# Adaptive modulation chunks summed on VectorE by 32x32 transposes, and a rotary turn by lane shuffle

## The chip, the cores and the metric

The kernel runs on one core of a Trainium2 chip. The metric is device time in microseconds of that core, as the median of several executions of the whole program. The engines are called PE (TensorE), DVE (VectorE), ACT (ScalarE), POOL (GpSimd) and SP (SyncE, which issues most DMAs). SBUF is the on-chip memory, PSUM (`bank`, 8 banks of 512 fp32 columns) is where TensorE writes. All data is fp32.

## The reference, cut to what matters

Two blocks of two layers each, over a sequence of 256 tokens and a width of 1024. In block one every layer is modulated by a vector that comes from a condition `c`:

```python
cond = jax.nn.silu(c)
for l in range(DEPTH):
    mod = cond @ ada_w[l] + ada_b[l]            # (1, 1024) @ (1024, 9216)
    sh1, sc1, g1, sh2, sc2, g2, sh3, sc3, g3 = jnp.split(mod, N_MOD, axis=-1)
    hn = _modulate(_rms_norm(h, norm_g[l, 0]), sh1, sc1)
    h = h + 0.5 * g1[:, None, :] * _swiglu(hn, ffn1_w_in[l], ffn1_w_out[l])
    hn = _modulate(_rms_norm(h, norm_g[l, 1]), sh2, sc2)
    z = hn @ w_in[l]
    ...                                         # attention, convolution, gating, projection with g2
    hn = _modulate(_rms_norm(h, norm_g[l, 2]), sh3, sc3)
    h = h + 0.5 * g3[:, None, :] * _swiglu(hn, ffn2_w_in[l], ffn2_w_out[l])
```

In block two the first 16 of the 64 columns of a head are rotated by position, for queries and keys of 18 of 24 heads:

```python
x1, x2, rest = t[..., :8], t[..., 8:16], t[..., 16:]
return jnp.concatenate([x1 * cos - x2 * sin, x2 * cos + x1 * sin, rest], axis=-1)
```

## The kernel before, in words

Activations lie with the channel on the partition and the token on the free axis, in 8 tiles of 128x256. A large product is done in three terms, since the matmul takes operands of a rounded fp32 type: a weight chunk comes by DMA into one of four slots of `ring`, ScalarE writes its rounded part `w_hi` (L1175), POOL the rest `w_lo` (L672), and TensorE multiplies `w_hi` by the rounded activation, `w_hi` by its rest and `w_lo` by the rounded one (`terms`, L706). A full chunk is 1 MB, 8 tiles of 128x256, and 48 matmuls of 256 columns. `w_hi` and `w_lo` hold two chunks. Each engine follows its own program; the order is written out by hand and tied by semaphores (`eng.step(mark)` counts, `eng.at(mark)` is waited on).

An FFN of block one has an input half of 11 pairs of chunks (`p`, gate and up, 96 matmuls) and an output half of 4 groups (`g`, 132 matmuls). For each pair ScalarE takes the silu (L1263), VectorE the product (L1642) and the rest of its rounded form (L1645). Pairs alternate between banks 0, 1 and 2, 3.

The modulation vector has 18 chunks of 512 columns in each layer, 2 MB of `ada_w` each. Chunks 0 to 3 of the first layer are done at the start. The others are spread over the FFNs by `ADA_AT`: in FFN 1, chunks 4 to 11 beside pairs 1 to 8 and 12 to 15 beside the groups of the output half; in FFN 2, chunks 16 and 17 and the next layer's 0 to 3 beside pairs 1 to 6 (in the last layer only 16 and 17). SP loads a chunk into one of two buffers (`ada_fill`, L530 and L531, behind the sum of the chunk two before). VectorE multiplies its 8 tiles by columns of `cond` and adds them (`partial_sum`, L1545, L1548, L1552), which leaves a sum over 128 partitions. `ada_reduce` (L813) does that on TensorE: four matmuls, each with 128 columns of the sum as the stationary operand and a column of ones as the moving one. The result stands in bank 7, one column for 128 channels, from where `modulation` (L1570) takes it when a group of columns is wanted. `ada_reduce` comes one pair behind the sum in the input half and behind the group in the output half.

Ahead of the projection z of block one, VectorE computes modulation columns 48 to 63, two gain vectors (`gated_scale`, L1629) and small tables (L1791 to L1803), while PE adds the squares of the residual (`norm_sum`, L800 and L803) and ScalarE takes the reciprocal root (L1209, L1211). Then `scale_norm` (L1614, L1623) normalises tile by tile.

In block two the first 13 units of the projection z2 run before the heads, 48 matmuls each. Ten of them are rotary units. ScalarE copies such a unit from PSUM to `raw` (L1456), PE multiplies it by a constant turning matrix (`rotate`, L1076, one fp32 matmul of 512 columns, behind the next unit), and VectorE takes the unit times cosine (L1939), the turned one times sine (L1941), adds them and stores queries or keys (L1945, L1951, L1957). A unit's bank is used again four units later.

Of the kernel before, what the change touches and what calls it, by code (L numbers as in the profile page):

```python
# [24 lines left out]
P = 128  # L25
D = 1024
S = 256
L = 2
# [29 lines left out]
def constant_tables():  # L58
# [14 lines left out]
    rot = np.zeros((P, P))  # L73
    for base in (0, 64):
        for j in range(8):
            rot[base + 8 + j, base + j] = -1
            rot[base + j, base + 8 + j] = 1
    put("rotate", rot)
# [5 lines left out]
    for base in (0, 64):  # L84
        for half in (0, 8):
            cos[base + half:base + half + 8] = np.cos(ang)
            sin[base + half:base + half + 8] = np.sin(ang)
# [35 lines left out]


# [108 lines left out]
def ada_chunk(phase, step, layer):  # L233
# [5 lines left out]
    return (layer, c) if c < ADA_CHUNKS else (layer + 1, c - ADA_CHUNKS)  # L239

# [139 lines left out]
def build(nc, dram, out, at, old):  # L380

    plan = Plan()
    with ExitStack() as ctx:
# [41 lines left out]
        ada_acc = view(ARENA - 2048, 2, ADA_COLS)  # L425
        wfx = view(ARENA - 2048, KT, P)
# [36 lines left out]
        raw, by_cos = view(20480, 2, 2 * S), view(20480 + 4 * S, 2, S)  # L463
# [223 lines left out]
        def _(pe):  # L687
# [127 lines left out]


# [47 lines left out]
            def ffn(s, layer, following):  # L864
                for p in range(PAIRS):
# [5 lines left out]
                    of = ada_chunk(s + "in", p - 1, layer)  # L871
                    if of:
                        ada_reduce(*of)
                for g in range(4):
# [5 lines left out]
                    of = ada_chunk(s + "out", g, layer)  # L880
                    if of:
                        ada_reduce(*of)
# [79 lines left out]
            for layer in eng.layers("one"):  # L962
# [4 lines left out]
                norm_sum("z")  # L967
                if layer == 0:
                    pe.wait_ge(params_in, 16 * n_params_total)
# [84 lines left out]
            for layer in eng.layers("two"):  # L1054
# [16 lines left out]
                def rotate(n):  # L1071

                    pe.wait_ge(scalar_done, eng.at(f"z2 out {ROTARY[n]}"))
                    if n >= 2:
                        pe.wait_ge(vector_done, eng.at(f"rotated {ROTARY[n - 2]}"))
                    mm(bank[:, 5 + n % 2], tab("rotate"), raw[:, n % 2, :], start=True, stop=True) \  # L1076
                        .then_inc(tensor_done, eng.step(f"rotary {ROTARY[n]}"))

                for p in range(BEFORE_HEADS):
                    z2_unit(p)  # L1080
                    if 1 <= p <= len(ROTARY):
                        rotate(p - 1)
# [64 lines left out]
        def _(act):  # L1147
# [296 lines left out]
            for layer in eng.layers("two"):  # L1444
                squares_and_norm(f"z2 {layer}", "z2")
                ahead[0] = 2
                def copy_out(p):
# [24 lines left out]
                for p in range(BEFORE_HEADS):  # L1472
                    round_to("z2", Z2_UNITS[p][1][-1] + 1)
                    copy_out(p)
# [568 lines left out]
```

## Time and profile before

| | us |
|---|---|
| median of 3 executions | 2115.06 |
| lowest, highest | 2114.36, 2117.67 |
| profiled execution | 2113.42 |
| its span, first to last instruction | 2111.6 |

| engine | busy us | share of the span |
|---|---|---|
| PE | 2029.1 | 96% |
| POOL | 1321.6 | 63% |
| ACT | 947.8 | 45% |
| DVE | 767.0 | 36% |

The core moved 398.19 MB by DMA, 189 GB/s in the mean over the span, and up to 358 GB/s in the slices near the start. The mean granted clock of TensorE was 0.986 of its full 2.4 GHz. Matmuls are pipelined, so the duration of one L706 record (0.28 us) is longer than the distance from one to the next (0.12 us); distances between starts tell the pace. An fp32 matmul leaves two records.

### The profile page before, as it was taken

The page shows a single profiled execution, that of the slowest core. Times are in us where ns is not written, and L with a number is a line of the kernel's source. Part 1 is how long each engine was busy: PE and PEld are TensorE (multiplying, and loading weights), DVE is VectorE, ACT ScalarE, POOL GpSimd, SP SyncE. Part 2 cuts the span into 40 slices and gives each one's busy share as a digit, 9 for nine tenths or more (in the row PEclk, how much of TensorE's full clock was granted, in tenths as well). Part 3 has the DMA queues.
Part 4 walks back from the last instruction along what each step waited for, and adds up shares of the span by engine and source line. Part 5 has one row for each costly group of instructions (what it writes and reads, how often), then busy time and mean ns, then how long its engine had stood idle before and what let it go on. Part 6 is the DMA issues. An engine that isn't in the chain of part 4 may idle for free.

```text
span 2111.6 us, 36596 instructions
## 1 busy us (share of the span) xinstructions
PE 2029.1 (96%) x15458; PEld 1945.8 (92%) x15458; DVE 767.0 (36%) x1643; ACT 947.8 (45%) x1487; POOL 1321.6 (63%) x612
## 2 busy tenths in 40 slices
PE   6999997999999999889999999999999999999998
PEld 3999996899999998779999999989999999989998
DVE  3553576352145356734112432133301432133311
ACT  2444454443454445434444345525544345525543
POOL 1877760377877786216787765506886764506885
PEclk8999999999999999999999999999999999999999
DMA  9997650686599775227555543336654543335552
GB/s 326 358 342 252 190 177 20 235 289 197 178 315 349 244 249 179 80 63 258 187 165 168 179 149 112 120 120 190 189 193 131 193 144 109 127 124 180 182 198 81
DMA packets 356788, 398.19 MB, mean 189 GB/s; under 512 B 8984, under 2 KB 318992, under 8 KB 356624
## 3 DMA queue, kind: packets, MB, share of 16 engines
q1 hardware_dynamic: 356464, 395.65, 57.1%
q8 instruction: 122, 2.00, 0.4%
q10 hardware_dynamic: 160, 0.20, 0.1%
q14 instruction: 42, 0.34, 0.1%
HBM read 394.77 MB, written 1.05 MB: 187 GB/s over the span
## 4 chain that ended last, share of the span: by engine, by line
PE 89%; DVE 4%; ACT 3%; SPq 1%; issue 1%; POOL 1%; DMA 1%; DVEq 0%; ACTq 0%
PE bank L706 70%; PE bank L790 5%; PE bank L1112 3%; PE bank L813 1%; PE bank L908 1%; PE bank L942 1%; POOL w_lo L672 1%; SPq L534 1%; PE bank L1076 1%; PE bank L697 1%; DVE arena L1685 1%; DVE bank L1614 1%; ACT arena L1311 1%; PE bank L737 1%; PE bank L741 1%
## 5 line engine op out<-in xcount | busy, mean ns | idle before, releaser
L672 POOL TENSOR_TENSOR w_lo<-ring,w_hi 128x1024 fp32r<-128x1024 f32 (+2 forms) x608 | 1321.4, 2198 | 770.2 <-ACT w_hi L1175 769.9
L706 PE MATMUL bank<-hn,w_hi 128*128 128x256 f32 x2752 | 793.6, 288 | 3.7 <-POOL w_lo L672 3.5
L706 PE MATMUL bank<-hn_lo,w_hi 128*128 128x256 f32 x2752 | 778.4, 283 | 0.0
L706 PE MATMUL bank<-hn,w_lo 128*128 128x256 f32 x2752 | 778.3, 283 | 0.0
L1175 ACT ACTIVATE w_hi<-ring 128x1024 fp32r<-128x1024 f32 (+2 forms) x608 | 576.1, 975 | 373.3 <-PE bank L706 337.1
L706 PEld LDWEIGHTS bank<-hn,w_hi 128*128 128x128 f32 x2752 | 527.5, 192 | 10.5 <-POOL w_lo L672 5.4
L706 PEld LDWEIGHTS bank<-hn_lo,w_hi 128*128 128x128 f32 x2752 | 527.7, 192 | 4.9 <-issue 4.3
L706 PEld LDWEIGHTS bank<-hn,w_lo 128*128 128x128 f32 x2752 | 527.5, 192 | 0.0
L706 PE MATMUL bank<-gated,w_hi 128*128 128x256 f32 x1408 | 249.7, 280 | 0.0
L706 PEld LDWEIGHTS bank<-gated,w_hi 128*128 128x128 f32 x1408 | 215.0, 187 | 0.0
L706 PE MATMUL bank<-gated,w_lo 128*128 128x256 f32 x704 | 196.4, 279 | 0.0
L706 PE MATMUL bank<-up,w_hi 128*128 128x256 f32 x1024 | 181.0, 280 | 0.0
L1548 DVE SCALAR_TENSOR_TENSOR bank<-arena,cond,bank 128x512 f32<-128x512 f32 x204 | 154.2, 756 | 7.3
L706 PEld LDWEIGHTS bank<-up,w_hi 128*128 128x128 f32 x1024 | 156.3, 187 | 0.0
L706 PE MATMUL bank<-up,w_lo 128*128 128x256 f32 x512 | 142.8, 279 | 0.0
L706 PEld LDWEIGHTS bank<-gated,w_lo 128*128 128x128 f32 x704 | 132.4, 188 | 0.0
L1642 DVE TENSOR_TENSOR bank<-arena,bank 128x512 f32<-128x512 f32 x44 | 30.6, 696 | 249.1 <-PE bank L706 249.1
L790 PE MATMUL bank<-arena,ring 128*128 128x256 f32 x512 | 114.7, 387 | 5.1 <-DVE arena L1975 3.2
L790 PEld LDWEIGHTS bank<-arena,ring 128*128 128x128 f32 x512 | 99.2, 195 | 20.3 <-DVE arena L1975 4.0
L1263 ACT ACTIVATE arena<-bank 128x512 f32<-128x512 f32 x44 | 26.3, 597 | 181.5 <-PE bank L706 180.9
L1311 ACT ACTIVATE arena<-arena,stat 128x128 f32<-128x128 f32 x120 | 53.2, 444 | 101.3 <-DVE stat L1699 44.0
L706 PEld LDWEIGHTS bank<-up,w_lo 128*128 128x128 f32 x512 | 96.3, 188 | 0.0
(199 smaller groups left out, 2241.3 us busy)
## 6 DMA issues: line engine op xcount, KB each, us to landing
ring<-in_ffn_w_in SPq DMA_DIRECT2D x88, 1024.0 KB, 6.7
ring<-in_w_in SPq DMA_DIRECT2D x72, 1024.0 KB, 5.2
arena<-in_ada_w SPq DMA_DIRECT2D x35, 2048.0 KB, 10.4
ring<-in_w_up SPq DMA_DIRECT2D x32, 1024.0 KB, 5.5
ring<-in_w_down SPq DMA_DIRECT2D x32, 1024.0 KB, 5.1
ring<-in_ffn_w_out SPq DMA_DIRECT2D x32, 768.0 KB, 4.7
ring<-in_ffn_w_out SPq DMA_DIRECT2D x32, 640.0 KB, 4.1
ring<-in_w_in SPq DMA_DIRECT2D x16, 512.0 KB, 3.6
```

What stands on the lines that cost most here:

```text
L534: sp.dma_start(dst, src).then_inc(rows_in, 16)
L672: pool.tensor_tensor(w_lo[:, q, ks], ring[:, r, k0:k0 + n], w_hi[:, q, ks], ALU.subtract) \
L697: i = pe.transpose(dst, src, ident[0:n, 0:n])
L706: last = mm(out, a, b, start=start and i == 0, stop=stop and i == 2)
L737: mm(outs[c], w_hi[:, q, kw, ws], hn[:, kx], start=kx == 0 and c == 0, stop=False)
L790: last = mm(outs[c], ring[:, s, k, c * P:(c + 1) * P], x[:, k0 + k, :], start=(k0 + k == 0), stop=(k0 + k == total - 1))
L1112: last = mm(b[:, c], ring[:, s, k0 + k, c * P:(c + 1) * P], o2[:, k0 + k, :], start=(k == 0), stop=(k == nk - 1))
L1175: f(w_hi[:, q, half * 4:half * 4 + n], ring[:, r, k0:k0 + n], ACT.Copy).then_inc(weights_rounded, 1)
L1263: f(act_tmp[:, j], bank[:, 2 * j], ACT.Silu).then_inc(silu_done, eng.step(f"{s} silu {p}", silu_done))
L1311: f(t, t, ACT.Exp, bias=st[:, b + j:b + j + 1], scale=scale, accum_out=st[:, 10 + 2 * m + j:11 + 2 * m + j]) \
L1548: stt(part, src[:, k], col(cond, k), part, ALU.mult, ALU.add).then_inc(vector_done, eng.step())
L1642: tt(bank[:, 2 * j], act_tmp[:, j], bank[:, 2 * j + 1], ALU.mult) \
```

## The change

It has two parts.

In the first, `ada_reduce` is gone for all chunks but the two of the start. VectorE ends a chunk's sum in PSUM, transposes it there in blocks of 32x32 (`dve.transpose`, 128x512), and adds each run of 32 columns (`tensor_reduce`, to 16 columns), which leaves for each of 4 groups of 32 partitions the channel on the partition and a partial sum. TensorE adds the four groups for a whole batch of chunks at once (`ada_fold`): four matmuls of 4n columns by a shifted window of a constant `fold`. There are three batches a layer: chunks 4 to 11 (fold behind pair 9 of FFN 1), 12 to 15 (behind the norm sum of z) and 16 to 21 (behind pair 8 of FFN 2). Modulation columns 48 to 63 and the gain vector of FFN 2 are computed behind the norm of z instead of ahead of it, and columns 64 to 71 at pair 9 of FFN 2 instead of pair 3. The wait on `ada_reduced` inside `partial_sum` is gone, and a wait on its own `ada_summed` ahead of the transpose is new.

In the second, the rotary matmul and the copy to `raw` are gone. VectorE turns a unit from bank to bank by `stream_shuffle` (lanes 0 to 7 and 8 to 15 of each 32 change places) and waits for the unit itself instead of the matmul; the sign is in the table `sin`. Lanes 32 to 47 of each 64 are shuffled too, where the sine is zero. The constant table grows by 192 columns.

```diff
-    put("rotate", rot)
+    put("fold", np.concatenate([np.zeros((P, 96)), r[:, None] % 32 == np.arange(32)[None, :], np.zeros((P, 96))], axis=1))
...
-            sin[base + half:base + half + 8] = np.sin(ang)
+            sin[base + half:base + half + 8] = np.sin(ang) * (1 if half else -1)
...
+ROTARY_LANES = [i + 8 if i < 8 else i - 8 if i < 16 else i for i in range(32)]
+ADA_BATCHES = ((4, 8), (12, 4), (16, 6))
...
+            def ada_fold(layer, batch):
+                c, n = ADA_BATCHES[batch]
+                if batch == 2 and layer + 1 == L:
+                    n = 2
+                last_c = c + n - 1
+                pe.wait_ge(vector_done, eng.at(f"ada columns {last_c}"))
+                place = c - ADA_FIRST
+                sums = ada_columns[:, 16 * place:16 * (place + n)].rearrange("p (x q) -> p q x", q=4)
+                for q in range(4):
+                    last = mm(bank[:, 7, 4 * c:4 * (c + n)], tab("fold", P, 96 - 32 * q), sums[:, q],
+                              start=(q == 0), stop=(q == 3))
+                last.then_inc(ada_reduced, 1)
...
-                    of = ada_chunk(s + "in", p - 1, layer)
-                    if of:
-                        ada_reduce(*of)
+                    if (s, p) in (("f1", 9), ("f2", 8)):
+                        ada_fold(layer, 0 if s == "f1" else 2)
...
-                    of = ada_chunk(s + "out", g, layer)
-                    if of:
-                        ada_reduce(*of)
...
                 norm_sum("z")
+                ada_fold(layer, 1)
...
-                def rotate(n):
-                    pe.wait_ge(scalar_done, eng.at(f"z2 out {ROTARY[n]}"))
-                    if n >= 2:
-                        pe.wait_ge(vector_done, eng.at(f"rotated {ROTARY[n - 2]}"))
-                    mm(bank[:, 5 + n % 2], tab("rotate"), raw[:, n % 2, :], start=True, stop=True) \
-                        .then_inc(tensor_done, eng.step(f"rotary {ROTARY[n]}"))
...
-                    if i in ROTARY:
-                        if p >= 2:
-                            act.wait_ge(tensor_done, eng.at(f"rotary {ROTARY[p - 2]}"))
-                        f(raw[:, p % 2], b, ACT.Copy).then_inc(scalar_done, eng.step(f"z2 out {i}"))
-                        return
...
-                if n >= 2:
-                    dve.wait_ge(ada_reduced, n - 1)
-                stt(ada_acc[:, n % 2], src[:, nk - 1], col(cond, nk - 1), part, ALU.mult, ALU.add).then_inc(ada_summed, 1)
+                stt(dst, src[:, nk - 1], col(cond, nk - 1), part, ALU.mult, ALU.add).then_inc(ada_summed, 1)
...
+                part, turned_ = bank[:, 5 + c % 2], bank[:, 6 - c % 2]
+                partial_sum(n, ada[:, c % 2], part, part)
+                dve.wait_ge(ada_summed, n + 1)
+                dve.transpose(turned_, part).then_inc(vector_done, eng.step())
+                dve.wait_ge(vector_done, eng.at())
+                dve.tensor_reduce(ada_columns[:, 16 * place:16 * (place + 1)],
+                                  turned_.rearrange("p (b r) -> p b r", r=32), AX.X, ALU.add) \
+                    .then_inc(vector_done, eng.step(f"ada columns {place + ADA_FIRST}"))
...
-                    if (s, p) == ("f2", 3):
+                    if (s, p) == ("f2", 9):
                         modulation(layer, 64, 72, (layer, 17))
...
-                modulation(layer, 48, 64, (layer, 15))
                 gated_scale(8, 32, R_NORM_G + 8).then_inc(vector_done, eng.step())
-                gated_scale(16, 56, R_NORM_G + 16).then_inc(vector_done, eng.step())
...
                 scale_norm("z", lambda k: col(der, 8 + k), 24)
+                modulation(layer, 48, 64, (layer, 15))
+                gated_scale(16, 56, R_NORM_G + 16).then_inc(vector_done, eng.step())
...
-                    dve.wait_ge(tensor_done, eng.at(f"rotary {i}"))
+                    dve.wait_ge(weights_used, eng.at(f"used z2 {Z2_UNITS[n][1][-1]}"))
...
+                    dve.stream_shuffle(bank[:, 5 + n % 2, 0:t * S], bank[:, n % 4, 0:t * S], ROTARY_LANES) \
+                        .then_inc(vector_done, eng.step())
```

## Rows read from the trace of the kernel before

**Rows 1.** The page, section 4: the chain that ended last, by engine.

```profile
PE 89%; DVE 4%; ACT 3%; SPq 1%; issue 1%; POOL 1%; DMA 1%; DVEq 0%; ACTq 0%
```

**Rows 2.** The chain in order of time: start us, us, what.

```profile
108.38 0.79 PE bank L813 x8
109.17 11.61 PE bank L706 x96
...
199.07 15.65 PE bank L706 x132
215.51 15.65 PE bank L706 x132
...
498.49 96.84 PE bank L706 x816
```

**Rows 3.** The chain again, before the heads of block two.

```profile
1168.36 0.86 PE bank L1076 x2
```

**Rows 4.** ScalarE's timeline: start us, us, line, tiles, idle before.

```profile
66.35 0.60 ACT L1263 ACTIVATE arena<-bank 128x512 f32<-128x512 f32 x1 [4.22 <-PE bank L706]
...
77.87 0.60 ACT L1263 ACTIVATE arena<-bank 128x512 f32<-128x512 f32 x1 [4.22 <-PE bank L706]
...
90.27 0.60 ACT L1263 ACTIVATE arena<-bank 128x512 f32<-128x512 f32 x1 [5.09 <-PE bank L706]
...
105.60 1.06 ACT L1175 ACTIVATE w_hi<-ring 128x1024 fp32r<-128x1024 f32 x1 [0.45 <-PE bank L706]
```

**Rows 5.** The chain inside the heads of block two.

```profile
1238.72 0.66 PE bank L908 x4
```

**Rows 6.** Timelines of PE, VectorE and ScalarE at the norm ahead of z.

```profile
252.21 0.36 PE L737 MATMUL bank<-hn,w_hi 128*128 128x256 f32 x1 [2.41 <-ACT hn L1235]
...
248.50 0.17 DVE L1570 TENSOR_TENSOR mod<-bank,arena 128x16 f32<-128x16 f32 x1 [0.37 <-PE bank L813]
...
248.87 0.23 DVE L1791 TENSOR_SCALAR der<-const,arena 128x4 f32<-128x4 f32 x1
...
251.07 0.88 DVE L1614 SCALAR_TENSOR_TENSOR bank<-h,der,bank 128x256 f32<-128x256 f32 x2
...
248.16 0.42 ACT L1203 ACTIVATE square<-h 128x256 f32<-128x256 f32 x1 [0.29 <-DVE h L1664]
...
250.34 0.39 ACT L1211 ACTIVATE bank<-rstd 128x256 f32<-128x256 f32 x1
```

**Rows 7.** VectorE's timeline, a rotary unit.

```profile
1182.54 0.69 DVE L1939 TENSOR_TENSOR arena<-bank,const 128x512 f32<-128x512 f32 x1 [3.13 <-PE bank L1076]
```

**Rows 8.** VectorE's timeline, a pair of 11.52 us with a chunk.

```profile
424.33 0.70 DVE L1642 TENSOR_TENSOR bank<-arena,bank 128x512 f32<-128x512 f32 x1 [3.13 <-PE bank L706]
...
435.85 0.70 DVE L1642 TENSOR_TENSOR bank<-arena,bank 128x512 f32<-128x512 f32 x1 [3.13 <-PE bank L706]
```

**Rows 9.** VectorE late, and the chain there.

```profile
448.95 0.17 DVE L1570 TENSOR_TENSOR mod<-bank,arena 128x8 f32<-128x8 f32 x1 [10.91 <-PE bank L813]
...
455.46 0.69 DVE L1642 TENSOR_TENSOR bank<-arena,bank 128x512 f32<-128x512 f32 x1
...
448.92 11.61 PE bank L706 x96
...
461.31 11.61 PE bank L706 x96
```

**Rows 10.** PE, PEld, DVE, ACT, POOL busy, clock, DMA share, GB/s; a load to landing.

```profile
84.00:134.00 50.00, 50.00 (x421) 50.00 (x421) 29.73 (x41) 20.83 (x25) 38.36 (x18) 1.00 1.04 348
...
461.30:473.70 12.40, 12.40 (x106) 12.40 (x106) 10.21 (x15) 5.22 (x7) 11.36 (x6) 1.00 1.07 368
...
ring<-in_ffn_w_in SPq DMA_DIRECT2D x1, 1024.0 KB, 12.5
```

**Rows 11.** POOL's timeline at the last rotary unit and behind it.

```profile
1707.09 4.74 POOL L672 TENSOR_TENSOR w_lo<-ring,w_hi 128x1024 fp32r<-128x1024 f32 x2 [1.84 <-ACT w_hi L1175]
1712.84 4.74 POOL L672 TENSOR_TENSOR w_lo<-ring,w_hi 128x1024 fp32r<-128x1024 f32 x2 [1.01 <-ACT w_hi L1175]
```

More of the change, by code:

```diff
@@ L72, in constant_tables @@
     put("group64", r[:, None] // 64 == r[None, :] // 64)
[L73 to L77, printed above, removed]
-    put("rotate", rot)
+    put("fold", np.concatenate([np.zeros((P, 96)), r[:, None] % 32 == np.arange(32)[None, :], np.zeros((P, 96))], axis=1))
     put("neg_suffix", -(r[:, None] >= r[None, :]).astype(np.float32))
@@ L239, in ada_chunk, with ada_batch @@
     return (layer, c) if c < ADA_CHUNKS else (layer + 1, c - ADA_CHUNKS)
+ADA_BATCHES = ((4, 8), (12, 4), (16, 6))
+def ada_batch(layer, c):
+    if c < ADA_FIRST:
+        layer, c = layer - 1, c + ADA_CHUNKS
+    b = 0 if c < 12 else 1 if c < 16 else 2
+    return c - ADA_FIRST, 2 + 3 * layer + b + 1
 def ada_column(c):
@@ L425, in build @@
         ada_acc = view(ARENA - 2048, 2, ADA_COLS)
+        ada_columns = view(ARENA - 2048, sum(n for _, n in ADA_BATCHES) * 16)
         wfx = view(ARENA - 2048, KT, P)
@@ L462, in build @@
         tile2, turned2 = view(20480, SLOTS, SCW), view(20480 + SLOTS * SCW, SLOTS, SCW)
-        raw, by_cos = view(20480, 2, 2 * S), view(20480 + 4 * S, 2, S)
+        by_cos = view(20480, 2, S)
         result, result_rows = view(0, KT, S), view(KT * S, 2, D)
@@ L1473, in _ @@
                     round_to("z2", Z2_UNITS[p][1][-1] + 1)
-                    copy_out(p)
+                    if Z2_UNITS[p][0] not in ROTARY:
+                        copy_out(p)
                 round_to("z2", BEFORE_HEADS + 3)
@@ L1540, in col, with partial_sum @@
                 return t[:, i:i + 1]
-            def partial_sum(n, src, part, nk=KT):
+            def partial_sum(n, src, part, dst):
+                nk = KT
                 ts(part, src[:, 0], col(cond, 0), None, ALU.mult).then_inc(vector_done, eng.step())
@@ L1558, in ada_sum @@
                 dve.wait_ge(vector_done, eng.at())
-                partial_sum(ada_sums(layer, c), ada[:, c % 2], bank[:, 5 + c % 2])
+                n, (place, _) = ada_sums(layer, c), ada_batch(layer, c)
+                part, turned_ = bank[:, 5 + c % 2], bank[:, 6 - c % 2]
[6 more added lines that the diff above has]
+                    .then_inc(vector_done, eng.step(f"ada columns {place + ADA_FIRST}"))
             def modulation(layer, first, last, summed):
@@ L1567, in modulation @@
                 else:
-                    dve.wait_ge(ada_reduced, ada_sums(*summed) + 1)
+                    dve.wait_ge(ada_reduced, ada_batch(*summed)[1])
                 at_ = MOD_TILES if first == 0 else first
@@ L1585, in _ @@
             dve.wait_ge(first_ada_in[0], 16)
-            partial_sum(0, first_ada[0], bank[:, 2])
+            partial_sum(0, first_ada[0], bank[:, 2], ada_acc[:, 0])
             dve.wait_ge(tensor_done, eng.at("rows turned"))
@@ L1601, in _ @@
             dve.wait_ge(first_ada_in[2], 16)
-            partial_sum(1, first_ada[2], bank[:, 3])
+            partial_sum(1, first_ada[2], bank[:, 3], ada_acc[:, 1])
             dve.wait_ge(vector_done, eng.at())
@@ L1938, in _ @@
                     t = 1 if half else 2
+                    dve.stream_shuffle(bank[:, 5 + n % 2, 0:t * S], bank[:, n % 4, 0:t * S], ROTARY_LANES) \
+                        .then_inc(vector_done, eng.step())
                     tt(by_cos[:, 0:t], src[:, 0:t], cosb[:, 0:t], ALU.mult) \
                         .then_inc(vector_done, eng.step(None if half else f"by cos {i}"))
+                    dve.wait_ge(vector_done, eng.at())
                     tt(rot[:, 0:t], rot[:, 0:t], sinb[:, 0:t], ALU.mult).then_inc(vector_done, eng.step())
```

2 lines of the change are left out of this document (removed).

## The prediction

> **What bounds the kernel now.** I read the page first: PE carries 89% of the chain that ended last [rows 1]. That is an average over stages, so the second view is the chain in order of time, and there the reader should look at the small entries between the long stretches of L706 matmuls. In the input half of an FFN each pair of chunks is 96 matmuls and then an entry of eight L813 records (four fp32 matmuls, two records each), and the next pair follows without a gap [rows 2]. Before the heads of block two each unit is 48 matmuls and then two L1076 records, one rotary matmul [rows 3], ten in each layer. Both kinds stand on the chain themselves. So TensorE is the bound in these stretches, and what is taken off its queue there should come off the time, unless the next resource is closer behind than it looks. The third step is to see how close: VectorE's timeline (adaptive sums), POOL's (weight split), and DMA.
>
> **Part 1, the adaptive reduces leave TensorE.** By the table of chunks (`ADA_AT`) 32 reduces go and 2, chunks 0 and 2 of the first layer, stay. Of the 32, 16 lie in the input half of FFN 1 (8 in each layer), 8 in its output half, 8 in the input half of FFN 2 (6 and 2). The price of one comes from the distance between equal events with and without it. ScalarE's silu of one pair follows that of the pair before after 77.87 - 66.35 = 11.52 us where no reduce lies between, and after 90.27 - 77.87 = 12.40 us with one; later ones are as the second [rows 4]. 96 matmuls at 0.12 us are 11.52, so a reduce costs 0.87 us, though each of its matmuls has one column. In the output half a group has 132 matmuls and comes every 215.51 - 199.07 = 16.44 us. Without a reduce, 816 matmuls take 96.84 us; 288 of them are of the input half (34.56 us), which leaves 62.28 / 528 = 0.118 each, 15.57 us for a group, and again 0.87 for the reduce [rows 2]. Two of the 32, the last ones of FFN 1, stand ahead of the norm sum and are part 3. The other 30 give 30 x 0.87 = 26.1 us.
>
> **Part 2, the folds that come in.** Each is four fp32 matmuls of at most 32 columns. The nearest rows on both sides are the 1-column reduce (0.87 us for four, 0.22 each) and a pair of fp32 matmuls of 256 and 128 columns, which takes 0.66 us, 0.33 the mean [rows 5]. Four of at most 32 columns then cost 0.87 to 1.3 us; 32 columns are nearer to one than to 192, so I take 0.87 for a fold. Four of the six stand between pairs (batches 0 and 2, both layers): 3.5 us. Their waits end early: chunk 11 is summed during pair 8 and its fold stands after pair 9. The other two stand behind the norm sum, where PE is idle for 2.41 us [rows 6]; they cost nothing, and 0.87 each if that idle time were gone.
>
> **Part 3, the norm ahead of z.** Now the last reduce goes first, then the norm sum, and VectorE waits 0.37 us for the reduce, then computes the modulation and two scales before the small tables. It reaches the first norm operation at 251.07, when the rstd has been ready since 250.73 [rows 6]. So VectorE is last there. Without the wait, the modulation and one scale, it goes from 248.13 (248.50 less the wait, the end of the last residual add) through one scale of about 0.15 us and the same 2.2 us of tables (248.87 to 251.07), to 250.5. The norm sum also loses the reduce in front of it; its last matmul then waits for the square that ends at 248.58, so the rstd comes some 0.5 us earlier and stays ahead of VectorE. Gain about 0.55 us in each layer, 1.1 us. What follows (the operations by k, the weight split behind them) is a chain that moves with it. The modulation and scale put behind the norm, 0.4 us of VectorE, are ahead of nothing that PE waits for at once.
>
> **Part 4, rotary.** Twenty matmuls of 512 fp32 columns go, 0.86 us each, all on the chain, and PE goes on with the next unit at once: 17.2 us [rows 3]. ScalarE also loses 20 copies of 0.6 us and stops waiting for the end of a unit before it rounds the next weights. VectorE gains a shuffle of 128x512 in each unit. No row shows one; its neighbours over the same tile take 0.69 us (a 512-column product from PSUM), and the ends are nothing and 2.27 us, from which it would fall behind: VectorE has 3.13 us of idle time behind a query unit, less the 0.86 by which a unit gets shorter [rows 7]. I take 0.7 us: under 1 us more in 5.75 us, and the units go over four banks, so no unit of PE waits. Cost nothing.
>
> **Part 5, what VectorE gains in the sums.** For each chunk a transpose of 128x512 and a reduce to 16 columns come in. No row has the transpose. The neighbour of that size is the product with 0.70 us [rows 8]; lower end nothing, upper end the idle time that hides it. That is in the one place where a pair already takes 11.52 us: the product at 424.33 and the next one at 435.85, with 3.13 us idle [rows 8]. I take 0.75 us each, 1.5 us against 3.13, so 1.6 us stay. Even lateness is forgiven: at 448.95 VectorE has sat for 10.91 us on a reduce, reaches the product only at 455.46, some 7 us after the pair ended, and the chain still shows pairs at 448.92 and 461.31, 12.39 apart [rows 9]. The change also removes this stall, for no gain, since PE did not feel it. The Trainium skill ("VectorE: DVE Perf Modes", the perf-mode tier table) says that the shuffle and the reduce have only the slowest mode, one element a cycle, which fits the value that I took from the neighbours; no run here shows either.
>
> **Part 6, is DMA close behind?** In layer 0 the pairs with a chunk move 348 GB/s for 50 us at a DMA share of 1.04; the highest window is 368 [rows 10]. The same bytes at 11.52 us a pair want 348 x 12.39 / 11.52 = 374 GB/s. So in layer 0 the supply can't quite follow. How much margin is there? A weight chunk issued at 91.67 lands after 12.5 us, 104.2; ScalarE rounds it from 105.60 [rows 4, 10]. PE multiplies by it only after 9 us more (second chunk of the pair that starts at 109.17), of which rounding and splitting a half need 1.06 and 2.37 [rows 4, 11]. Margin 1.4 us at ScalarE and about 5 more behind. At 368 a pair takes 348 x 12.39 / 368 = 11.72 us, 0.2 too long, 1.6 us in eight pairs: hidden. At an unchanged 348 it is 0.87 a pair, 7.0 in eight, of which the margin takes most. I take 0.5 us, ends 0 and 7.0.
> The Trainium skill ("SBUF — State Buffer", the table of bandwidths beside the two sides of SBUF) gives about 358 GB/s for HBM to a core. By that figure a pair with a chunk, 4.19 MB, would take 11.71 us, 4.6 us more in 24 pairs: 2078.7, inside rival (a). The trace has a window at 368, above it, so the rows decide.
>
> **Sum**: -26.1 + 3.5 - 1.1 - 17.2 + 0.5 = -40.4 us. The profiled execution took 2113.42 us (2111.6 span), 1.6 below the median of 2115.06. 2113.4 - 40.4 = 2073.0 for such an execution, 2074.6 as a median.
>
> **Rivals.** (a) *DMA becomes the bound in the pairs with chunks.* For: the share above 1 in layer 0. Against: 11.52 us pairs stand at the start of layer 0 [rows 4]. At 348 GB/s all eight pairs of layer 0 give back 7.0 us: 2081.1. With 0.2 us also in the 16 others it is 2084.3.
> (b) *POOL becomes the bound.* It splits a chunk in 4.77 us; at 5.76 us a chunk it idles 1.01 us instead of 1.84 [rows 11]. For: 4.77 of 5.76 us is 83%. Against: that row is from a stretch that already runs at full pace, and it does not hold PE. If each of the 24 pairs and 20 units kept 0.2 us of it: +8.8, 2083.4.
> (c) *Slower than before: VectorE becomes the bound of every pair with a chunk.* Place: transpose and reduce in L1548's loop. They must take more than 3.13 us together to make the pair longer than 11.52. To lose all 40 us in 24 pairs they need 1.7 us more in each, 4.8 us together, 2.4 us for an operation whose neighbours take 0.7. At 6.0 us it is 24 x 2.9 = 70 us: 2144. I see nothing for it but that the transpose has no row.
> (d) *The change does not do what it says*: the removed matmuls had been filling time in which PE would wait for the next split anyway. Then nothing comes of the 20 rotary matmuls, and the result is 2091.8. Against: POOL's idle time of 1.84 us in each rotary unit waits for ScalarE, and ScalarE for PE [rows 11, 4].
>
> **Chances.** Forecast 0.74; (a) 0.12; (b) 0.08; (c) 0.02; (d) 0.04. The forecast's own spread is 3 us around it: 0.05 us in each of 54 measured distances is 2.7 us, and the fold's upper end is 1.7. Below I double it, since the later phases all start at another time. Range 2068.5 to 2084.5: its upper end takes in (a) and (b), (c) and (d) are left out. Faster by over 0.2% (4.2 us, about what a measurement of this kernel can tell from no change) is everything but (c) and an unforeseen remainder: 0.97; within 0.2% 0.01; slower 0.02.
>
> **What would show it.** Pairs with a chunk at 11.5 us between silus (12.4 if DMA or POOL holds them); units before the heads at 5.75; L1076 gone; six folds of about 0.9 us, two in idle time; transpose and reduce at 0.7 to 0.8 each, shuffle at 0.7; the first norm operation of z about 0.5 us earlier behind the last add; no waits of ScalarE for ring loads between 60 and 160 us. A new PE wait on L672 inside pairs would speak for (b), ScalarE's waits for DMA for (a), and VectorE without idle time before L1642 for (c).

## The result, and the profile after

| | before | after |
|---|---|---|
| median, us | 2115.06 | 2061.88 |
| lowest, highest | 2114.36, 2117.67 | 2060.0, 2062.39 |
| profiled execution, its span | 2113.42, 2111.6 | 2062.2, 2060.4 |
| granted TensorE clock | 0.986 | 0.981 |

The ratio is 0.9745 (95% interval 0.9728 to 0.9762): 53.2 us less. The forecast was 40.4 less, with a lower end of 2068.5. The time lies 12.7 us below the forecast and 6.6 us below the range.

The page of after, the engines' busy time and the chain by engine:

```profile
PE 1981.9 (96%) x15210; PEld 1905.0 (92%) x15210; DVE 826.5 (40%) x1747; ACT 939.7 (46%) x1467; POOL 1320.9 (64%) x612
...
PE 88%; DVE 4%; ACT 3%; POOL 1%; issue 1%; SPq 1%; DMA 1%; DVEq 0%; ACTq 0%
```

PE was and is the bound [rows 1]. VectorE gained 59.5 us of busy time (767.0 to 826.5), and its share of the chain stayed at 4%.

The chain of after in order of time (start us, us, what):

```profile
56.79 109.44 PE bank L716 x912
166.22 0.82 PE bank L837 x8
167.04 71.44 PE bank L716 x624
...
499.39 82.97 PE bank L716 x720
```

L716 is what L706 was. Where [rows 2] had 96 matmuls, a reduce of 0.79 us, and 96 again, there are now 912 without a gap, one fold (L837), and 624.

ScalarE's timeline of after, the silus of three pairs, and VectorE's over one pair with a chunk and one rotary unit (start us, us, line, tiles, idle before):

```profile
91.38 0.60 ACT L1275 ACTIVATE arena<-bank 128x512 f32<-128x512 f32 x1 [4.22 <-PE bank L716]
102.90 0.60 ACT L1275 ACTIVATE arena<-bank 128x512 f32<-128x512 f32 x1 [4.22 <-PE bank L716]
114.42 0.60 ACT L1275 ACTIVATE arena<-bank 128x512 f32<-128x512 f32 x1 [4.22 <-PE bank L716]
```

```profile
71.08 0.73 DVE L1571 STREAM_TRANSPOSE bank<-bank 128x512 f32<-128x512 f32 x1
71.85 0.69 DVE L1573 TENSOR_REDUCE arena<-bank 128x16 f32<-128x512 f32 x1
74.17 0.70 DVE L1658 TENSOR_TENSOR bank<-arena,bank 128x512 f32<-128x512 f32 x1 [1.63 <-PE bank L716]
...
1139.59 0.01 DVE L1955 LOAD_MASK_SELECT bank<-bank  x1 [3.37 <-PE bank L716]
1139.61 0.70 DVE L1955 STREAM_SHUFFLE bank<-bank 128x512 f32<-128x512 f32 x1
...
1145.35 0.01 DVE L1955 LOAD_MASK_SELECT bank<-bank  x1 [1.53 <-PE bank L716]
```

Pairs with a chunk come every 11.52 us (12.40 in [rows 4]), with 1.63 us of VectorE's idle time left of the 3.13 in [rows 8]. Rotary units come every 5.76 us. Behind a query unit VectorE still waits 1.53 us for PE, where it was 3.13 us in [rows 7]: the unit got 0.85 us shorter and VectorE has the shuffle besides. Behind a key unit it was 4.59 and is 2.99.

So the removed work left as forecast. What is new is in stretches whose code the change doesn't touch. In the down projection of block two 768 matmuls multiply `up` by the weights in one unbroken run. The last pieces of the chain that hold it (the up projection's end and the down projection, 1488 matmuls), of before and of after:

```profile
1445.29 176.86 PE bank L706 x1488
...
1922.90 176.86 PE bank L706 x1488
```

```profile
1408.83 173.46 PE bank L716 x1488
...
1875.05 173.46 PE bank L716 x1488
```

And 85 us inside the down projection, which runs from 1531.5 to 1622.2 before and from 1495.1 to 1582.3 after. First before, then after (window, PE, PEld, DVE, ACT, POOL busy with their counts, granted clock, DMA share, GB/s):

```profile
1532.00:1617.00 85.00, 85.00 (x724) 85.00 (x723) 6.77 (x14) 35.26 (x40) 73.39 (x32) 1.00 0.53 172
```

```profile
1496.00:1581.00 85.00, 85.00 (x753) 85.00 (x752) 6.71 (x15) 35.60 (x40) 74.85 (x33) 1.00 0.55 176
```

PE is busy throughout and the granted clock is 1.00 (2.4 GHz) in both, yet 753 matmuls fit where 724 did. (Both counts take in two that had begun before the window. Paces are therefore taken from the starts of the 768: 117.8 ns from one to the next before, 113.4 after.) The output halves of the FFNs, which multiply `gated`, show the same step. That is 528 matmuls in each of four FFNs and 768 in each of two down projections, 3648 in all, at 4.4 ns each: 16 us. The miss is 12.7.

### The profile page after: what moved, and what is told of

It is laid out like the page before. It is cut to its first block, busy times and chain, and to the rows that moved or that the text cites. A ratio compares the mean times of both kernels' runs of the same rounds, so it can differ in the third digit from the quotient of the medians.

```text
span 2060.4 us, 36118 instructions
## 1 busy us (share of the span) xinstructions
PE 1981.9 (96%) x15210; PEld 1905.0 (92%) x15210; DVE 826.5 (40%) x1747; ACT 939.7 (46%) x1467; POOL 1320.9 (64%) x612
## 3 DMA queue, kind: packets, MB, share of 16 engines
HBM read 394.82 MB, written 1.05 MB: 192 GB/s over the span
## 4 chain that ended last, share of the span: by engine, by line
PE 88%; DVE 4%; ACT 3%; POOL 1%; issue 1%; SPq 1%; DMA 1%; DVEq 0%; ACTq 0%
PE bank L716 70%; PE bank L800 6%; PE bank L1124 3%; POOL w_lo L682 1%; PE bank L963 1%; PE bank L929 1%; SPq L544 1%; DVE arena L1701 1%; DVE bank L1630 1%; ACT arena L1323 1%; PE bank L707 1%; PE bank L751 1%; PE bank L747 1%; ACT w_hi L1187 1%; PE bank L1025 1%
## 5 line engine op out<-in xcount | busy, mean ns | idle before, releaser
L716 PE MATMUL bank<-hn,w_hi 128*128 128x256 f32 x2752 | 786.3, 286 | 3.3 <-POOL w_lo L682 2.9
L716 PE MATMUL bank<-hn_lo,w_hi 128*128 128x256 f32 x2752 | 778.6, 283 | 0.0
L716 PE MATMUL bank<-hn,w_lo 128*128 128x256 f32 x2752 | 778.6, 283 | 0.0
L716 PEld LDWEIGHTS bank<-hn,w_hi 128*128 128x128 f32 x2752 | 527.9, 192 | 7.1 <-POOL w_lo L682 5.3
L716 PEld LDWEIGHTS bank<-hn_lo,w_hi 128*128 128x128 f32 x2752 | 528.0, 192 | 1.1 <-issue 0.5
L716 PEld LDWEIGHTS bank<-hn,w_lo 128*128 128x128 f32 x2752 | 527.9, 192 | 0.0
L716 PE MATMUL bank<-gated,w_hi 128*128 128x256 f32 x1408 | 239.6, 276 | 0.0
L716 PEld LDWEIGHTS bank<-gated,w_hi 128*128 128x128 f32 x1408 | 212.0, 188 | 0.0
L716 PE MATMUL bank<-gated,w_lo 128*128 128x256 f32 x704 | 194.3, 276 | 0.0
L716 PE MATMUL bank<-up,w_hi 128*128 128x256 f32 x1024 | 174.2, 276 | 0.0
L716 PEld LDWEIGHTS bank<-up,w_hi 128*128 128x128 f32 x1024 | 154.1, 188 | 0.0
L716 PE MATMUL bank<-up,w_lo 128*128 128x256 f32 x512 | 141.3, 276 | 0.0
L716 PEld LDWEIGHTS bank<-gated,w_lo 128*128 128x128 f32 x704 | 132.1, 188 | 0.0
L1323 ACT ACTIVATE arena<-arena,stat 128x128 f32<-128x128 f32 x120 | 53.2, 444 | 102.7 <-DVE stat L1715 44.0
L716 PEld LDWEIGHTS bank<-up,w_lo 128*128 128x128 f32 x512 | 96.1, 188 | 0.0
```

Source lines behind the costliest of these rows:

```text
L716: last = mm(out, a, b, start=start and i == 0, stop=stop and i == 2)
L1323: f(t, t, ACT.Exp, bias=st[:, b + j:b + j + 1], scale=scale, accum_out=st[:, 10 + 2 * m + j:11 + 2 * m + j]) \
```

## The experiments

What could make identical matmuls faster? The change widens the constant table from 3863 to 3959 columns, 96 more. (The section on the change above says 192, which is wrong: `fold` brings 96 + 32 + 96 = 224 and `rotate` takes 128 away.) The tiles of a partition lie behind each other, so the arena, which holds `gated` and `up`, starts 384 bytes further on: at 128832 instead of 128448. Within 256 bytes that is 64 instead of 192. The weights (`w_hi` at 49280, `w_lo` at 65664, the stationary operands) and the normed residual (`hn` at 90240, `hn_lo` at 98432, a moving operand as `gated` and `up` are) all start at 128 within 256 and don't move.

The theory: the matmuls that remain got faster by where their operand starts, and the removed work is worth 40 us. The rival: the freed engines (ScalarE without copies, PE without interruptions) make them faster, so both gains are the change's own.

**Placement alone**, in the kernel before:

```diff
+    put("unused", np.zeros((P, 96)))
```

> The kernel before, with 96 unused columns of zeros at the end of the constant table and nothing else. They move all that is allocated behind the table, the arena with gated and up2 among it, by 384 bytes in each partition, as the change's wider table does. Placement theory: the matmuls whose moving operand lies in the arena (output halves of the FFNs and the down projection) are issued every 0.1134 us instead of 0.118, which is 2.4 us in each of four FFN output halves and 3.4 in each of two down projections, 16.4 us together: 2098.7. Rival (the gain of those stretches comes from what the change took off the other engines or off TensorE's queue): 2115, the down projection stays at 178.5 us between its two norms.

Measured 2102.49 (2101.72 to 2103.49), ratio 0.9941 (0.9927 to 0.9956): 12.5 us less with no instruction changed. The chain of this kernel:

```profile
748.65 15.65 PE bank L707 x132
765.10 15.07 PE bank L707 x132
780.95 15.65 PE bank L707 x132
...
1440.33 173.46 PE bank L707 x1488
```

The 173.46 us of after are here too, to the hundredth. The excess comes back without the change, so the freed engines are not what makes this stretch faster. In the output half of FFN 1 only every other group of 132 is faster (15.07 us, 15.65 otherwise). The groups are those between two adaptive reduces, which this kernel still has. The time was 3.8 us short of what was expected of it. The four slow groups of both layers are 2.3 us of that; another 1.2 us is a longer z stretch in layer 0 (147.5 to 148.6), whose cause was not looked for.

**The change, with the arena put back** to 192 within 256 bytes, by 128 unused bytes ahead of it:

```diff
+        sb("unused", 32)
```

> The changed kernel with 128 unused bytes in each partition ahead of the arena. The arena then starts at 192 modulo 256 as in the kernel before, but not at its place modulo 512 or 1024. Placement theory with a period of 256 bytes: the output halves go back to 0.118 us a matmul, 2061.9 + 16.4 = 2078.3. Placement with a longer period: another pace, or 2061.9. Rival without placement: 2061.9.

Measured 2075.02 (2073.78 to 2077.56), ratio 0.9814 (0.9797 to 0.983): 40.0 us less than before. The sum was 40.4. (The arena starts 512 bytes behind its place in the kernel before, at 128960, so it does stand at its old place modulo 512, other than the expectation has it, and at a new one modulo 1024.) Its chain has the old length again:

```profile
1884.18 176.86 PE bank L717 x1488
```

**One part alone.** Two kernels with the placement of before (the second has it within 256 bytes). The first is the kernel before with only the rotary part:

```diff
-                    mm(bank[:, 5 + n % 2], tab("rotate"), raw[:, n % 2, :], start=True, stop=True) \
...
+                    dve.stream_shuffle(bank[:, 5 + n % 2, 0:t * S], bank[:, n % 4, 0:t * S], ROTARY_LANES) \
```

> The kernel before with the rotary part of the change alone; the turning matrix stays in the constant table unused, so nothing moves in SBUF. By my sum for rotary, 20 matmuls of 0.86 us: 2115.1 - 17.2 = 2097.9. If POOL or VectorE took over a part there: 2100 to 2106. If removing the copies and waits of ScalarE were worth more than the matmuls (the 12 us that my sum lacks): 2086.

Measured 2101.02 (2098.27 to 2101.13), 14.0 us less; ratio 0.9931 (0.9916 to 0.9946). The stretch of z2 with its heads is 8.1 us shorter in each layer (299.1 to 291.0), 16.2 in all, against 17.2 in the sum. Some of it was given back: FFN 1 of layer 0 and the z stretch of layer 1 are 2.2 and 2.8 us longer in this profile, at a lower granted clock (0.983 over the span against 0.986).

The second is the changed kernel with only the sums. Its rotary matmuls are back, but it leaves out the turning matrix: they multiply by another table of that size (`group64`), so its queries, keys and result are not those of the reference. It is here for its times alone:

```diff
-ROTARY_LANES = [i + 8 if i < 8 else i - 8 if i < 16 else i for i in range(32)]
...
+        sb("unused", 32)
...
+                    mm(bank[:, 5 + n % 2], tab("group64"), raw[:, n % 2, :], start=True, stop=True) \
```

> The adaptive sums of the change alone, with the arena at 192 modulo 256 as in the kernel before. The rotary matmuls are back; their matrix is another table of the same size, so that nothing moves, and rotated queries and keys are wrong. By my sum (26.1 for the reduces, 1.1 at the norms of z, less 3.5 for the folds and 0.5 for DMA): 2115.0 - 23.2 = 2091.8. If the parts overlap with each other or with placement, it differs from 2115.0 less the difference of the other two kernels at the old place (2101.0 and 2075.0), which is 2089.0.

Measured 2094.54 (2092.02 to 2096.75), 19.4 us less; ratio 0.9902 (0.9886 to 0.9919). By stage, between the reciprocal roots of the norms: FFN 1 of layer 1 is 9.0 us shorter (by the sum 11 reduces less one fold, 8.7), FFN 2 of layer 0 4.2 (6 less one fold, 4.4), FFN 2 of layer 1 1.2 (2 less one fold, 0.9). The whole is 3.8 us short of the sum, and the missing time is in stretches at a lower clock again (0.981 over the span).

The two parts alone give 33.4 us, both together 40.0. In the three profiles the gap lies in FFN 1 of layer 0 (5.1 us) and the z stretch of layer 1 (5.4 us), and nowhere else by more than 1 us. In the one the granted clock was 0.963 and 0.962 with one part and 0.977 with both, in the first 104 us of the other 0.935 against 0.951. Whether the lower clock is by chance of the execution or comes with one part alone was not told apart, so that the parts simply add up is shown to some 7 us only.

**Which placement matters?** The first idea was the place of the moving operand as such: fast at 64 within 256 bytes, whatever else lies where. Then `hn`, which feeds the other two thirds of the large matmuls, should gain too:

```diff
-        hn, hn_lo = sb("hn", KT, S, dtype=F32R), sb("hn_lo", KT, S, dtype=F32R)
...
+        hn, hn_lo = sb("hn", KT, S, dtype=F32R), sb("hn_lo", KT, S, dtype=F32R)
```

The new line stands just ahead of the arena.

> The changed kernel with hn and hn_lo allocated just ahead of the arena instead of behind h, so that they start at the arena's place modulo 1024; the arena does not move. The matmuls of the input halves, of z, z2 and up have hn as moving operand and are issued every 0.120 us. Placement theory: they go to the arena's 0.1134, about 9100 of them, 60 us: near 2002. If the place of the stationary operand or the order of the three terms sets their pace: unchanged, 2061.9.

Measured 2033.12 (2019.41 to 2037.83), ratio 0.9603 (0.9566 to 0.9639): 82 us less than before and 29 less than after, by moving two tiles. It is the fastest version that was run. Its executions spread over 18 us, where those of before and after spread over 3.3 and 2.4. It is also 31 us above what was expected of it: in its trace many stretches run at 117.8 ns, among them the output halves of three FFNs, whose `gated` stands just where it does in after.

This fits two readings: the place of the moving operand, or its distance from the stationary one (here 64 - 128, which is 192 within 256). To tell them apart, the weights move to 64 as well, and `hn` stays at 128 within 256:

```diff
-        w_hi, w_lo = sb("w_hi", 2, 8, 256, dtype=F32R), sb("w_lo", 2, 8, 256, dtype=F32R)
...
+        w_hi, w_lo = sb("w_hi", 2, 8, 256, dtype=F32R), sb("w_lo", 2, 8, 256, dtype=F32R)
```

Here too the new line stands just ahead of the arena.

> The changed kernel with w_hi and w_lo, the stationary operands, allocated just ahead of the arena; hn and the arena keep their places modulo 1024. Modulo 256 the weights then start at 64, hn at 128, the arena at 64. If the distance between moving and stationary operand modulo 256 counts: input halves (distance 64, as the arena's in the kernel before) at 117.8 ns a matmul, output halves and down projection (distance 0, as hn's until now) at 120.0: 2062 - 20 + 24 = 2066. If the place of the moving operand alone counts: 120.0 and 113.4 as in the changed kernel, 2062.

Measured 2064.19 (2063.15 to 2065.99), ratio 0.9764 (0.9749 to 0.9778). `gated` and `up` stand where they do in after, at 64, but now at distance 0, and they went from 113.4 to 120.0 ns. `hn`, still at 128, went from 120.0 to 117.8, the pace that `gated` and `up` had at that distance (64) in the kernel before. The place alone is refuted; the distance stands. The next kernel asks the same without moving the weights, with the arena at 128, again distance 0:

```diff
+        sb("unused", 16)
```

> The changed kernel with 64 unused bytes ahead of the arena, which then starts at 128 modulo 256 as hn and the weights do. Placement theory, in either form: the output halves and the down projection are issued every 120.0 ns as the input halves are, 3648 matmuls x 6.6 ns = 24 us more: 2086. Without a period of 256 bytes: another pace.

Measured 2082.98 (2082.83 to 2083.13, two executions), ratio 0.9852 (0.9832 to 0.9871), 21 us above after where 24 were expected. 90 us of its down projection (which starts at 1505.85):

```profile
1505.00:1595.00 90.00, 90.00 (x752) 90.00 (x751) 6.77 (x14) 35.73 (x40) 75.99 (x33) 1.00 0.51 166
```

By the starts it is 120.0 ns in the down projection and in all four output halves. The chain piece of 1488 takes 178.56 us there, so the untouched stretch has had three lengths, 178.56, 176.86 and 173.46, by the placement alone.

**Other distances** for all large matmuls, `hn` and arena together: 128, 160 and 224 (the tile `small` ahead of them cut by 64 and by 32 bytes, or 32 bytes put in).

```diff
-        small = sb("small", 64)
+        small = sb("small", 48)
```

> The changed kernel with hn and hn_lo just ahead of the arena and a small tensor cut by 64 bytes, so that hn and the arena both start at 0 modulo 256 and the weights at 128: a distance of 128, the one class not seen yet. Distance theory says that hn and arena matmuls get the same pace, and not which. 113.3 throughout gives about 2002, 117.8 about 2058, 120.0 about 2086. A mix of paces, as in the kernel with hn moved, lies between.

> As the kernel before this one, at 32 modulo 256: a distance of 160, between 128 and 192. By steps of 64 it is 118.7 (2067) or as 192 (2033); by steps of 32 a pace of its own.

> The changed kernel with hn and hn_lo just ahead of the arena and 32 unused bytes in front of them: both moving operands start at 96 modulo 256, the weights at 128, a distance of 224. The classes seen so far are 0 (120.0 ns a matmul), 64 (117.8), 128 (118.7) and 192 (113.3, in places 117.8). If the pace goes by steps of 64 bytes, 224 belongs with 192 or 0: near 2033, or 2085. If it goes by 32: a pace of its own, perhaps 113.3 without the slow places, which would be about 2005.

Measured 2067.07 (2065.62 to 2072.5), 2061.46 (2059.24 to 2063.51) and 2062.86 (2062.4 to 2063.82); ratios 0.9781 (0.9767 to 0.9796), 0.9741 (0.9725 to 0.9757) and 0.9752 (0.9737 to 0.9766). The paces are 118.7 ns and in places 120.0, 117.3 or 118.7, and 118.3, so steps of 32 bytes count too. None comes near the 2033 of distance 192.

**Is the gain of placement apart from that of the change?** The kernel before, with its operands placed as in the fastest version:

```diff
+    put("unused", np.zeros((P, 96)))
...
-        hn, hn_lo = sb("hn", KT, S, dtype=F32R), sb("hn_lo", KT, S, dtype=F32R)
...
+        hn, hn_lo = sb("hn", KT, S, dtype=F32R), sb("hn_lo", KT, S, dtype=F32R)
```

> The kernel before with nothing of the change but its placement and more: 96 unused table columns, and hn and hn_lo just ahead of the arena, all moving operands at a distance of 192 from the weights. If the change's own work is worth 40 us at this placement too, it comes to the changed kernel's 2033 plus 40: 2073. If part of the 40 us hangs on the slow pace of TensorE (POOL or VectorE become the bound when TensorE is faster), the difference is smaller: 2050 to 2065.

Measured 2074.13 (2064.59 to 2079.18), ratio 0.9799 (0.9766 to 0.9831). Placement alone gives the kernel before 40 us, and the change at that placement gives another 41 (2074.1 to 2033.1). At the old placement it gave 40.0. So far as this can be told, the two add up: the executions of both kernels spread over 15 to 18 us, and by the intervals the 41 may be 10 us more or less. Four chain pieces of this kernel, each 96 matmuls between two reduces:

```profile
628.77 11.41 PE bank L707 x96
640.98 10.99 PE bank L707 x96
652.75 11.41 PE bank L707 x96
664.96 10.99 PE bank L707 x96
```

The pace changes at each reduce and back at the next, with one placement throughout. So at distance 192 there are two paces, 113.3 and 117.8 ns, and something other than the placement chooses. In this trace, of the kernel's slowest execution, 117.8 has most of the long stretches.

**The fastest version again**, same kernel, to see whether the choice belongs to the kernel or to the execution:

> The same program as the changed kernel with hn moved, whose executions lay between 2019 and 2038 us and whose trace has stretches of 113.3 and of 117.8 ns a matmul at one and the same placement. If the program fixes which stretch has which pace, the trace is as the first one and the spread comes from elsewhere. If the pace of a stretch is set anew in each execution, other stretches are at 117.8, and their number of matmuls times 4.5 ns makes up the difference of the two times.

Measured 2033.12 (2027.81 to 2038.44, two executions), ratio 0.9611 (0.9548 to 0.9675). First the earlier profile, then this one, 85 us of the same down projection:

```profile
1464.00:1549.00 85.00, 85.00 (x752) 85.00 (x752) 6.73 (x15) 35.34 (x40) 75.11 (x33) 1.00 0.53 178
```

```profile
1475.00:1560.00 85.00, 85.00 (x724) 85.00 (x724) 5.33 (x12) 33.01 (x37) 72.83 (x32) 1.00 0.53 171
```

And the chain piece that holds it, of the earlier and of this one:

```profile
1381.35 168.67 PE bank L716 x1488
```

```profile
1387.12 175.27 PE bank L716 x1488
```

752 matmuls against 724, by the starts 113.3 and 117.8 ns: same kernel, same places, same clock. Both layers' up and down projections were fast in the one and slow in the other: 2 x 6.6 = 13.2 us of the 19.0 between the two spans (2017.6 and 2036.6). The output half of FFN 1 in layer 0 has 528 matmuls x 4.5 ns, 2.4 us, of it, and the first units of z2 in layer 0 another 1.7. So the program doesn't fix the pace, and it holds through unbroken runs of many hundreds of matmuls. The two profiles are also of two different chips. That each chip has a pace of its own does not fit, since the executions on the one spread over 18 us and on the other over 11, but no two traces of one chip were compared. What makes the choice was not found.

## Why the prediction was right in its parts and wrong in its sum

**The failed step** is in the sentence that takes 0.118 us for each matmul of an output half [rows 2] and, behind it, in every part: the sum has terms for what goes and what comes in, and none for what stays. It took for granted that the matmuls that stay keep their pace. The section on the change names the cause itself, the wider constant table, and the prediction did not ask what lies behind that table. The missing term is -13.1 us (2075.02 to 2061.88), the whole miss of 12.7 and 0.4 more. With the arena at its old place within 256 bytes the same code gives 40.0 where the sum has 40.4. The 13 us are luck: nobody chose the width of the table for them, and with the arena 128 bytes further on the gain is 40.0, with 64 bytes 31.0.

A second error is in the range. Its 3 us of own spread came from the roundings of measured distances and from the fold. No bound was set for "the same matmul at another pace", though the prediction itself uses two: 0.12 us in the input half and 0.118 in the output half (119.8 and 117.8 ns from the starts). In the down projection before, the clock was 1.00 at 117.8 ns, as it was at 0.12 us in the pairs [rows 10], so the clock does not explain the difference; it was used and not asked about.

The sum's own terms, by what the runs showed, come to -26.1 + 3.5 - 1.4 - 16.2 + 0 = -40.2. They come this close in part because small errors cancel: 1.0 us too much for rotary, 0.3 too little for the norms and 0.5 for DMA that cost nothing.

**Part 1, reduces:** held. 11.52 us a pair, and 9.0 us in FFN 1 of layer 1 where the sum has 8.7.

**Part 2, folds:** held at its lower end, 0.88 us for 0.87 (0.87 to 1.3). The chain shows a fold of 32 columns with 0.82 us and a reduce of one column with 0.79 [rows 2], but both are shorter there than in the distances between events. Two silus with a fold between them, in after:

```profile
160.50 0.60 ACT L1275 ACTIVATE arena<-bank 128x512 f32<-128x512 f32 x1 [4.22 <-PE bank L716]
172.90 0.60 ACT L1275 ACTIVATE arena<-bank 128x512 f32<-128x512 f32 x1 [5.10 <-PE bank L716]
```

That is 12.40 us, 0.88 more than 11.52 and as with a reduce. The folds at the norm sum cost nothing, as said. PE's timeline of after there:

```profile
240.05 0.96 PE L837 MATMUL bank<-arena,const 128*128 128x16 f32 x8
242.38 0.35 PE L747 MATMUL bank<-hn,w_hi 128*128 128x256 f32 x1 [1.38 <-ACT hn L1247]
```

**Part 3, the norm ahead of z:** the gain is 0.70 us and not 0.55, and of the two that can come last, VectorE's tables and ScalarE's root, it is now the other. VectorE's and ScalarE's timelines of after:

```profile
239.54 0.15 DVE L1809 TENSOR_TENSOR small<-const,arena 128x4 f32<-128x4 f32 x1
...
241.24 0.88 DVE L1630 SCALAR_TENSOR_TENSOR bank<-h,der,bank 128x256 f32<-128x256 f32 x2 [0.97 <-ACT bank L1223]
```

```profile
240.75 0.39 ACT L1223 ACTIVATE bank<-rstd 128x256 f32<-128x256 f32 x1
```

From the last residual add (ends 239.00) to the first norm operation it is 2.24 us, before 2.94 [rows 6]. The tables took less time than forecast, VectorE is ready 0.97 us early, and the root is what comes last. The 2.2 us of tables that the prediction carried over held a product of four columns that took 1.20 us before; the same product (L1809 above) took 0.15 in after. Before, on VectorE and on POOL:

```profile
249.26 1.20 DVE L1795 TENSOR_TENSOR small<-const,arena 128x4 f32<-128x4 f32 x1
```

```profile
249.18 1.26 POOL L672 TENSOR_TENSOR w_lo<-ring,w_hi 128x512 fp32r<-128x512 f32 x1 [0.89 <-ACT w_hi L1175]
```

It began 0.08 us behind one of POOL's splits and ended 0.02 behind it, in layer 1 too; in after it falls between two splits. So 1.05 us of that term was a meeting with POOL that the change moved away. It is a small term with a small error.

**Part 4, rotary:** 8.1 us a layer for 8.6. The shuffle takes 0.70 us, as taken from its neighbours, and hides: 1.53 us of idle time are left behind a query unit, for 2.27 less 0.7.

**Part 5, the sums on VectorE:** 0.73 and 0.69 us for 0.75 each, and 1.63 us of idle time left for the 1.6 forecast. The product is never late now, and the 10.91 us of [rows 9] are gone for nothing, as said. By the Trainium skill ("VectorE: DVE Perf Modes", the perf-mode tier table) shuffle and reduce move one element a cycle; both took what the one-element neighbours take, 0.70 and 0.69 us, so the trace agrees.

**Part 6 and rival (a), DMA:** the window that [rows 10] show for before, in after:

```profile
84.00:134.00 50.00, 50.00 (x419) 50.00 (x418) 36.54 (x52) 21.92 (x26) 41.94 (x18) 1.00 1.05 348
```

The rate stayed at 348 GB/s, not at the 374 that the faster pairs want. The supply caught up later (from 160 to 180 us it is 272 GB/s, 176 before), the margin took the delay, and the pairs stayed at 11.52. The wait of ScalarE for the ring, over the stretch from 40 to 250 us (us in total, times, longest):

```profile
ACT w_hi L1187 <- DMA ring<-in_ffn_w_in: 0.5, 1, 0.5
```

It is one wait, at 151.97, in a place where ScalarE waits 0.45 us for PE in every other pair. So it cost ScalarE 0.05 us and PE nothing (912 matmuls without a gap). That it reads 0.5, the number that the sum took, is chance. Rival (a) is out.

**Rival (b), POOL:** the pairs with a chunk stand at 11.52 us and the rotary units at 5.76, so POOL held neither; out. (Its row has 4.74 us for a chunk, not the 4.77 of the text.) **Rival (c), slower by VectorE:** out by the 1.63 us of idle time. **Rival (d):** out by the kernel with rotary alone.

**The clock** took a little back in this execution. The stretches of FFN 1 and of the following z in layer 0, before and then after (columns as above):

```profile
18.00:250.00 232.00, 224.41 (x1767) 210.25 (x1765) 111.09 (x178) 94.53 (x125) 163.10 (x80) 0.98 0.91 303
250.00:397.00 147.00, 129.03 (x800) 116.51 (x800) 87.12 (x246) 67.92 (x135) 53.19 (x25) 0.95 0.33 103
```

```profile
18.00:240.00 222.00, 214.64 (x1677) 199.11 (x1676) 128.02 (x202) 94.45 (x124) 162.05 (x79) 0.96 0.94 315
240.00:391.00 151.00, 134.40 (x809) 119.99 (x808) 87.77 (x246) 68.22 (x135) 54.18 (x25) 0.92 0.32 103
```

The granted clock is 0.02 to 0.03 lower, with more of the time at 1.2 GHz, and the z stretch got 3.7 us longer (147.46 to 151.14 between the roots) although its norm got shorter. In layer 1 it is 147.50 for 148.41. The kernel with the arena put back has the same code, and its clock in the 222 us of FFN 1 was 0.977 for 0.962, so the lower clock does not belong to the code of the change. That kernel also shows where the 3 us stay by which the placement gained less in the time (13) than by count (16): against that kernel FFN 1 of layer 0 lacks 2.8 us of what its 528 matmuls should gain and the z stretch behind it is 2.4 us longer, while that of layer 1 is 1.0 shorter. The prediction had no term for it.

## What to carry to other kernels

A change to a constant, a table or a tile moves everything allocated behind it, so before its gain is explained, compare the pace of a long stretch that the change does not touch, and run the kernel before with the same padding. A sum of removed work needs a line for the work that stays: if two stretches of equal instructions show different distances at the same clock, find out why before using either. And where matmuls bound the kernel, try a few placements of the moving operand against the stationary one: here that was worth as much (some 40 us) as the rewriting, though not in every execution alike.

## What the runs showed of the hardware

The distance from one 256-column matmul to the next, at a granted clock of 1.00 and with PE never idle, depended on where the moving operand starts relative to the stationary one. All are starts in a partition, taken within 256 bytes; that 256 is the period rests on distance 0, which is 0 within 512 for `hn` in the kernel before and 256 within 512 for the arena put 64 bytes on, with 120.0 ns in both; for the other distances a multiple of 256 was not told apart. Worked out from the starts of unbroken runs of `hn`, `gated` or `up` matmuls:

| distance, bytes | ns a matmul |
|---|---|
| 0 | 120.0 |
| 64 | 117.8, in some stretches 113.3 |
| 128 | 118.7, in some stretches 120.0 |
| 160 | 117.3 or 118.7 |
| 192 | 113.3 or 117.8 |
| 224 | 118.3 |

All but the first two rows were seen at one place of the weights only (128). At 192 both paces occur in one execution, change at an interruption (an adaptive reduce), and differ between executions of one kernel. Distances 64 and 192 show the same two paces and differ in how often: at 64 it was 117.8 in all stretches but a few short ones, at 192 often 113.3. Why the distance matters, and what chooses between the two paces, stays open: the records show start and duration, not what TensorE waits for. By the Trainium skill ("TensorE: Matmul & The Clock Gate", section "Wait — 56ns, not 53.3ns?") the distance between matmuls back to back is the column count over 2.4 GHz and about 2.5 ns, an estimate of 109.2 ns for 256 columns. No stretch here came below 113.3, and at distance 0 it was 10% above that estimate. That section doesn't speak of a weight load for each matmul, which every one here has (15210 of each in after), nor of where operands start.

An fp32 matmul of few columns costs by its being one: four of one column took 0.87 us of PE [rows 4], four of 32 columns 0.88, by the distance between silus, where one of 512 columns took 0.86. A VectorE product of 128x4 took 0.15 us alone and 1.20 where it began just behind a POOL operation, ending with it; what held it was not asked. And a VectorE transpose of 128x512 fp32 from PSUM to PSUM in blocks of 32 took 0.73 us, no more than an addition over the same tile.
